# Decoder block with a PEER layer: two small tiles of the retrieval moved from PSUM to SBUF, and the tables that order its side work replaced

## The reference

```
h = h + (sigmoid(ga) * (a @ W_a) + sigmoid(gb) * (b @ W_b)) @ W_out
h = h + PEER(RMSNorm(h));  return RMSNorm(h)

q = (xt @ w_q).reshape(T, 8 heads, 2, 128);  s = einsum('thpd,hpnd->thpn', q, sub_keys)
s1, i1 = top_k(s[:, :, 0], 16);  s2, i2 = top_k(s[:, :, 1], 16)      # of 128 keys each
cand = s1[..., :, None] + s2[..., None, :]                            # 16 x 16
top_s, pos = top_k(cand, 16);  idx = i1 * 128 + i2 taken at pos;  gates = softmax(top_s)
y = sum over the 8 x 16 chosen experts e of  gate_e * gelu(u_e . x) * v_e
```

## Time and profile before

| | us |
|---|---|
| median of three runs | 1688.71 |
| the three runs | 1690.17, 1688.36, 1688.71 |
| the profiled execution, its own time | 1690.17 |
| its span, first to last instruction | 1688.4 |
| PE busy in the span | 1674.1 |
| DVE, ACT, POOL busy in the span | 1234.8, 780.1, 773.8 |

### The profile page before, as it was taken

How to read it: one execution, slowest core, us unless ns; L and a number is a source line. 1 busy time by engine, 2 the same in 40 slices (tenths; PEclk the granted TensorE clock), 3 DMA queues, 4 the chain that set the end, 5 groups by cost and what they waited for, 6 DMA issues and landing times.

```text
span 1688.4 us, 24662 instructions
## 1 busy us (share of the span) xinstructions
PE 1674.1 (99%) x9069; PEld 1477.8 (88%) x9069; DVE 1234.8 (73%) x2291; ACT 780.1 (46%) x1379; POOL 773.8 (46%) x484
## 2 busy tenths in 40 slices
PE   9999999999999999999999999999999999999998
PEld 6788877788888999999999999999888888888887
DVE  7977636744524899999986575744888888888886
ACT  5533326544212343467766767733333333333334
POOL 4545322434334878765555577774222322222220
PEclk9999999999999999999999999999999999999999
DMA  8322432374334899978777699997999999999993
GB/s 224 101 75 63 113 91 60 94 240 140 113 119 146 304 302 328 323 260 308 252 277 256 248 361 363 398 390 246 352 370 350 374 349 371 354 358 364 356 360 124
DMA packets 258639, 433.68 MB, mean 257 GB/s; under 512 B 14736, under 2 KB 181904, under 8 KB 256856
## 3 DMA queue, kind: packets, MB, share of 16 engines
q1 hardware_dynamic: 202648, 249.12, 45.4%
q0 software_dynamic: 36864, 134.23, 21.0%
q10 hardware_dynamic: 19008, 48.77, 7.8%
HBM read 372.82 MB, written 59.24 MB: 256 GB/s over the span
## 4 chain that ended last, share of the span: by engine, by line
PE 58%; DVE 7%; issue 2%; ACT 1%; DMA 0%; POOL 0%; ACTq 0%; DVEq 0%
PE bank L251 17%; PE bank L253 17%; PE bank L252 17%; PE bank L1764 5%; DVE lists L1538 1%; DVE rows L1259 1%; DVE slot L1587 1%; DVE lists L1576 1%; DVE lists L1582 0%; DVE top_i L1536 0%; ACT hot L1441 0%; DVE top_i L1548 0%; DVE pair_i L1548 0%; DMA rows<-in_u_rows,expert 0%; DVE pair_i L1536 0%
## 5 line engine op out<-in xcount | busy, mean ns | idle before, releaser
L246 POOL TENSOR_TENSOR spl_a<-raw,spl_a 128x1024 fp32r<-128x1024 f32 x170 | 409.7, 2412 | 333.9 <-ACT spl_a L242 332.7
L242 ACT ACTIVATE spl_a<-raw 128x1024 fp32r<-128x1024 f32 x296 | 313.1, 1059 | 388.9 <-PE bank L253 383.8
L251 PE MATMUL bank<-act,spl_a 128*128 128x384 f32 (+1 forms) x1216 | 426.2, 351 | 1.8 <-PEq L1181 1.7
L253 PE MATMUL bank<-act,spl_a 128*128 128x384 f32 (+1 forms) x1216 | 418.1, 344 | 0.0
L252 PE MATMUL bank<-act,spl_a 128*128 128x384 f32 (+1 forms) x1216 | 417.7, 344 | 0.0
L251 PE MATMUL bank<-spl_a,aws 128*128 128x512 f32 x768 | 298.9, 389 | 0.0
L253 PE MATMUL bank<-spl_a,aws 128*128 128x512 f32 x768 | 298.8, 389 | 0.0
L252 PE MATMUL bank<-spl_a,aws 128*128 128x512 f32 x768 | 298.8, 389 | 0.0
L1250 POOL DMA_INDIRECT rows<-in_v_tab,expert x128 | 135.1, 1055 | 347.2 <-DVE hot L1656 336.9
L251 PEld LDWEIGHTS bank<-act,spl_a 128*128 128x128 f32 x1216 | 229.1, 188 | 12.3 <-issue 3.6
L252 PEld LDWEIGHTS bank<-act,spl_a 128*128 128x128 f32 x1216 | 229.1, 188 | 7.7 <-issue 0.7
(11 more groups left out here) (316 smaller groups left out, 2386.1 us busy)
## 6 DMA issues: line engine op xcount, KB each, us to landing
raw<-in_u_t SPq DMA_DIRECT2D x128, 512.0 KB, 4.9
raw<-in_v_tab SPq DMA_DIRECT2D x128, 512.0 KB, 7.5
dense_gates<-mixbuf ACTq DMA_DIRECT2D x12, 2048.0 KB, 8.8
mixbuf<-dense_gates SPq DMA_DIRECT2D x32, 768.0 KB, 9.3
gelu_ux<-gl ACTq DMA_DIRECT2D x120, 192.0 KB, 5.5
mixbuf<-gelu_ux SPq DMA_DIRECT2D x30, 768.0 KB, 12.2
raw<-in_w_in SPq DMA_DIRECT2D x44, 512.0 KB, 3.9
raw<-in_w_q SPq DMA_DIRECT2D x16, 512.0 KB, 4.1
```

The costliest lines, as they stand in the source:

```text
L242: eng.activation(spl(n, 0, slice(0, W)), raw[:, s, :], ACT.Copy).then_inc(hi_done, 1)
L246: eng.tensor_tensor(spl(n, 1, slice(0, W)), raw[:, n % RAW, :], spl(n, 0, slice(0, W)).bitcast(F32), ALU.subtract).then_inc(lo_done, 1)
L251: nc.tensor.matmul(out, w_hi, x_hi, start=first, stop=False)
L253: return nc.tensor.matmul(out, w_lo, x_hi, start=False, stop=last)
```

## The change

It has three parts.

**Tiles.** `top_v0` and `top_v1` become one tile `top_v` in SBUF, and `gsum` is an SBUF tile too. `rank`, `key_f` and the constant `iota` stay in bank 3.

**Tables.** `EXP_AT`, `SLOTS_AT`, `GATHER_AT` have other numbers. `QUAD_AT` is replaced by the function `quad_chunk`, which is asked in the same four places. The list of gathers has 134 entries instead of 128: gathers 128 to 133, the first six rows of v, now stand in iterations 121 to 124 of the u phase. The last gather of u moves from chunk 118 to 119.

**Place of `normalise`.** It is called at x = 3 of `fill` instead of x = 2.

```diff
-            top_v1 = sb(ctx, "top_v1", [P, 2, TOPK])
+            top_v = sb(ctx, "top_v", [P, 2, 2, TOPK])
+            gsum = sb(ctx, "gsum", [P, 2, PH])
...
-            top_v0 = bank[3][:, P + 8 * TOPK:P + 10 * TOPK].rearrange("p (a k) -> p a k", a=2)
-            gsum = bank[3][:, P + 10 * TOPK:P + 10 * TOPK + 2 * PH].rearrange("p (s h) -> p s h", s=2)
...
-            EXP_AT = [18, 39, 61, 87]
-            SLOTS_AT = [None, 41, 63, 92]
-            GATHER_AT = [4, 4, 4, 5, 5, 5, 6, 9, 10, 11, 12, 13, 14, 15, 16, 18, 19, 20, 20, 21, 23, 24, 25, 25,
...
-                         118, 118]
+            EXP_AT = [22, 45, 67, 89]
+            SLOTS_AT = [None, 47, 70, 90]
+            GATHER_AT = [6, 6, 6, 7, 8, 8, 10, 11, 13, 14, 15, 16, 17, 18, 20, 21, 22, 23, 24, 25, 26, 27, 28, 28,
...
+                         119, 121, 121, 122, 123, 123, 124]
...
-            QUAD_AT = [47, 48, 49, 49, 50, 50, 51, 52, 52, 53, 54, 54, 55, 55, 56, 57, 58, 58, 59, 60, 60, 61, 62,
...
+            def quad_chunk(q):
+
+                if q < 32:
+                    return 51 + 22 * q // 32
+                return 74 + 17 * (q - 32) // 32 if q < 64 else 91 + 3 * (q - 64) // 4
...
-                        if QUAD_AT[q] != j:
+                        if quad_chunk(q) != j:
...
-                        if QUAD_AT[q] == j + 1:
+                        if quad_chunk(q) == j + 1:
...
-                    if m % 4 == 0 and m and x == 2:
+                    if m % 4 == 0 and m and x == 3:
                         normalise(m // 4 - 1)
...
-                    top16([((top_v0, top_v1)[side][:, a, :], top_i[:, a, side, :], scb[:, m % PAIRS, a, side, :])
+                    top16([(top_v[:, a, side, :], top_i[:, a, side, :], scb[:, m % PAIRS, a, side, :])
...
-                                           top_v0[:, :, :].unsqueeze(3).to_broadcast([P, 2, TOPK, TOPK]),
-                                           top_v1[:, :, :].unsqueeze(2).to_broadcast([P, 2, TOPK, TOPK]),
+                                           top_v[:, :, 0, :].unsqueeze(3).to_broadcast([P, 2, TOPK, TOPK]),
+                                           top_v[:, :, 1, :].unsqueeze(2).to_broadcast([P, 2, TOPK, TOPK]),
```

## The result

The kernel after takes 1699.47 us (median of 6 runs, 1692.43 to 1700.51); the kernel before, run beside it, 1688.62 (1688.36 to 1690.17). The ratio is 1.0058, with a 95% interval of 1.0041 to 1.0075. So it is slower, by 10.9 us. The forecast was 1690.4 in a range up to 1695.5: the time lies above it, by 9.1. The profiled execution of the kernel after took 1700.25, with a span of 1698.4 against 1688.4 before. All 10 us come between the start of the u phase and its end, which moves from 1153.6 to 1163.7.

The account below looks back on a forecast made before the run. PE's own work was taken as the bound, with DVE close behind. Losses of 3.4 + 0.8 + 0.9 = 5.1 us against 3.4 before gave +1.7: 1691.9 profiled, 1690.4 median, range 1687.2 to 1695.5.

Parts of the forecast that it names:

- the chain: Chunks 67 to 81: tile 2's exponential, normalise and L1562 waits set DVE's pairs 13 to 15, making quad 47 late for PE.
- the forecast's 5.1: Forecast lost time after the change: 3.4 + 0.8 + 0.9 us, against 3.4 lost before.
- 728 at the latest against 730 for chunk 47's product. The 1.8 us go.: Chunk 47: normalise's needed exponential ends by 728, before PE's product at 730, so chunk 41's loss of 1.8 us vanishes.
- Up to 2.4 when a split has just begun: L1562 and L1614, twenty calls: each waits up to 2.4 us for a split; half meet one, 1.3 each, 13 us total.
- 1.9 and 0.7: Pairs 13 and 14, behind chunks 73 and 78: L1562's forecast waits for POOL's splits, in us.
- Its list of instructions: The tiles: only L1562, sixteen times, and L1614, four times, were said to get two SBUF operands.
- The term for chunk 81: Chunk 81: PE waits 3.4 us for quad 47, scaled by 917.7 where PE is ready at 914.3.
- 0.8 for quad 54: Pair 15: quad 54 is ready at 941.5 where PE wants it at 940.7, so PE waits 0.8 us.
- 0.9 behind it: Chunk 89's exponential with two table loads stands among the quads: a loss of 0.9 us, as the third wait before.
- The six gathers of v: Chunks 91 to 127: gathers ahead of splits have some 10 us of cover before chunk 126, so cost 0.
- DVE is later still: Rival, chunks 74 to 91: longer waits of L1562 and L1614 delay PE, +6.3 us, 1695; chance 0.34.
- The rival of the table switch: Rival: a longer ACT table switch ends chunk 67's exponential 1.4 us later, delaying normalise; +3.1, 1691.8; chance 0.04.

Follow-up runs that it names:

- experiment 1: Kernel before with top_v and gsum in SBUF, old tables and old place of normalise; 1700.72 us, ratio 1.0066.
- experiment 2: Kernel after with both tiles back in PSUM, so new tables and normalise at x = 3 only; 1688.29 us, ratio 0.9997.
- experiment 7: Kernel before with gsum alone moved to SBUF; 1694.03 us, ratio 1.0029.
- experiment 4: Kernel after with only gsum back in PSUM, top_v staying in SBUF; 1691.19 us, ratio 1.0008.
- Experiment 5: Kernel after with the transposes of tile 1 behind chunk 50 instead of 47; 1700.45 us, ratio 1.0059.
- experiment 10: Kernel before with gsum in SBUF, plus a 128 x 1 memset on POOL behind every gather of u; 1694.92 us, ratio 1.0032.
- experiment 9: Kernel before with gsum in SBUF, plus two gathers of u one iteration later, behind their splits; 1693.35 us, ratio 1.0024.
- Experiment 6: Kernel before, no new tile, with the transposes of tile 1 behind chunk 40 instead of 41; 1695.48 us, ratio 1.0039.
- experiment 3: Kernel after with only top_v0 back in PSUM, gsum staying in SBUF; 1687.93 us, ratio 0.9991.
- experiment 11: Kernel after plus a 128 x 1 memset on POOL behind every gather of u; 1699.16 us, ratio 1.0051.

## Why the prediction was wrong

Its mechanism was the right one: the two operands in SBUF wait for POOL's splits (experiments 1, 2, 7), and PE pays at quad 47. The place and the chain hold, as experiment 4 shows where nothing else disturbs them (3.07 lost at chunk 81, forecast 3.4). Three steps failed, and the first made most of the error: chunks 47 and 48 lost 7.5 us where the sum had nothing, and chunk 82 another 2.0, of the 9.5 by which the 14.6 exceed the forecast's 5.1.

**"728 at the latest against 730 for chunk 47's product. The 1.8 us go."** This step bounded `normalise(1)` by the exponential alone, and took from before that DVE would be in front of it by 724. The exponential was indeed early, ready at 723.7. DVE wasn't. The tables alone start that pair at 709.0 (experiment 2), 8.3 later than before; L1562 had by then been lengthened eight times, by 13.5 us together, and L1614 once by 2.6; some of it fell into DVE's waits for rows of u, and 11.2 was left: 720.2. Then two more waits, 1.5 and 2.6, came between that start and the transposes. I had summed DVE's waits (13 us) but charged them only to chunks 74 to 90, where I had argued that DVE is tight. The earlier trace rows showed DVE at 97.6 of 100 us ahead of chunk 41 already. Experiment 5 shows that it was no matter of one hand-over: asked three chunks later, DVE is late all the same. Chunk 47 was forecast to win 1.8 and lost 5.5.

**"Up to 2.4 when a split has just begun", 1.3 on average.** Measured: up to 2.8 more for L1562 (3.48 in all), 1.14 on average over its sixteen where half a chance of 1.3 gave 0.65; L1614 2.6 twice. The average is no constant either: 0.9 in experiment 4, 0.3 in experiment 1. The step took it that DVE waits only for a split that is already running, as its one row had it. The trace after and experiments 7 and 10 show that DVE also waits for the split that follows a gather without a pause, if it begins during the gather. L1614's 2.6 at chunk 47, half of what PE waited there, is of this kind, and so are the two longest L1562 before it. The Trainium skill, "SBUF — State Buffer", section "Who interferes with whom", says, where it speaks of DVE's 2-port modes, that whoever issues first gets the shared port pair and the other is blocked for the whole instruction, and for contention at large that issue order decides who is blocked. The trace agrees for a split already running (experiment 9), but not here: L1614 was first by 0.38 us at 730.59 and by 0.51 at 707.70 (experiment 7), and waited. These leads are by the trace's spans, which are rough on POOL.

The sum also has two slips in this step that nearly cancel. It took 2.4 - 0.2 + 0.16 as the extra time, which is the whole length of a waiting instruction, so L1562's own 0.68 should have come off; and L1562 ends 0.55 after the split, not 0.16. That 1.9 and 0.7 came out as 1.94 and 0.62 in experiment 4 is partly luck.

Its list of instructions was not right either. L1536, L1538 and L1548 (FIND_INDEX8 and MATCH_REPLACE8) now read `top_v` and another SBUF tile in 192 calls, 96 before. It cost nothing: the longest took 0.31, though 129 of them began during a split. Each has a MATCH_VALUE_LOAD in front, which reads the eight values in an instruction of its own. In the other direction, an instruction with one SBUF input did wait: the CAST of L1598 takes 0.18 in three of its four calls and 2.31 at 580.07, ending 0.03 after a split.

**The clock, which is in no term.** Lost time was counted at full pace behind each wait. After the waits of 5.1 and 2.4 the next chunk lost 2.05 and 2.00, and quad 47's own matmuls another 0.8. Experiment 6 isolates it: 1.82 behind a wait of 5.8. The trace of before had it to see at the start of the u phase, where matmuls behind an idle stretch start 0.32 apart, and the prediction passed over it (1.66 at chunk 0 in the table). Together 5 of the 10 us are this, as far as the split can be read; the waits of 1.62 and 0.45 before show none.

The term for chunk 81, 3.4, measured 3.9 (2.7 waiting, 1.2 mostly clock); 0.8 for quad 54 was nothing; 0.9 behind it was 0.76. The six gathers of v cost nothing, as forecast: no wait of PE is listed at chunk 126. The rival "DVE is later still" came nearest, but was given a place, 74 to 91, and a ceiling of +6.3. The range's ends, 1687.2 and 1695.5, aren't quite its own sums, 1687.0 and 1695.0; nothing hangs on that. The rival of the table switch has nothing for it: in the kernel after, ACT's exponential at 723.37 again starts 0.01 after its table load, and `normalise` didn't wait for it.

**Open.** Of 25 timed executions of the kernel after, 5 took 1692.4 to 1693.8 and 20 took 1697.8 to 1702.7. A gap of that size is about one long wait with its clock (7.5 at chunks 47 and 48), so perhaps L1614 sometimes misses the split, as in experiments 3 and 4. That is argued, not shown: none of the shorter ones was profiled. Why one call of L1562 in experiment 4 (655.40, 0.33 into a gather) took only 0.68 isn't settled either.

## What to carry to other kernels

Before a scratch tile moves from PSUM to SBUF, list which two-operand instructions of DVE (here TENSOR_TENSOR) thereby get both inputs from SBUF, and as the worst case charge each with the whole run of POOL's instructions that may follow without a pause. Charge every delay to the nearest request of PE first, and ask for each moved hand-over when its producer's engine gets there, not only when its input is ready. A wait of PE of 2.4 us or more cost 0.7 to 2.8 more behind it here.

## What the runs showed of the hardware

- L1614 and L1562, TENSOR_TENSORs with two SBUF inputs, take their usual 0.29 and 0.68 when they begin while POOL is in a gather and POOL pauses behind it (978.35 and 839.33 in the kernel after). When a split follows without a pause, they last until 0.16 (L1614) or 0.55 (L1562) after the end of the split: 2.9 to 3.5 us in the eight cases of the kernel after and of experiments 7 and 10, and so in the ten of experiments 1, 5 and 11. The one exception is the call of experiment 4, above. FIND_INDEX8 and MATCH_REPLACE8 don't wait (0.31 at most). A 128 x 1 memset between gather and split doesn't let them in (experiments 10 and 11). In experiment 1 one instruction waited 3.58 through splits that ran back to back:

```profile
572.36 3.58 DVE L1593 SCALAR_TENSOR_TENSOR expert_f<-slot 128x32 f32<-128x32 f32 x1
```

```profile
568.77 7.11 POOL L246 TENSOR_TENSOR spl_a<-raw,spl_a 128x1024 fp32r<-128x1024 f32 x3
```

- Behind waits of PE of 2.4 to 5.8 us, 3 to 17 matmuls started 0.32 apart, and the chunk behind lost 0.7 to 2.8 us; behind the waits of 0.45 to 1.6 of the kernel before none did. Between 1.6 and 2.4 no wait was measured.
